# The rounded copy of the attention core moves to ScalarE, with other rearrangements, in an encoder trunk of feed-forward, attention and recurrent layers

## What is computed

```python
for layer in range(2):
    g = norm_gains[layer]
    h = h + 0.5 * rms_norm(swiglu(rms_norm(h, g[0]), ffn_w_in[layer, 0], ffn_w_out[layer, 0]), g[1])
    hn = rms_norm(h, g[2])
    m = attention_mixer(hn, ...) if layer == 0 else recurrent_mixer(hn, ...)
    h = h + rms_norm(m, g[3])
    h = h + 0.5 * rms_norm(swiglu(rms_norm(h, g[4]), ffn_w_in[layer, 1], ffn_w_out[layer, 1]), g[5])
return h[:, 16:]
```

## Time and profile before

| | |
|---|---|
| median of 3 runs | 1040.99 us (1040.65 to 1041.19) |
| the profiled execution | 1041.22 us, of which the span is 1039.3 us |
| PE busy | 1023.8 us, 99% |
| DVE, ACT, POOL busy | 708.7, 562.5, 64.0 us |
| granted TensorE clock | 0.999 |
| read from HBM, written | 167.82 MB, 1.05 MB |

### The profile page before, as it was taken

The page is one execution under the profiler, slowest core; times in us unless marked ns, Lnnn a source line. Parts: engine busy times, 40 slices in busy tenths (PEclk is TensorE's granted clock), DMA queues, the critical chain, the costliest instruction groups (busy, mean ns, idle before and its releaser), DMA issues. The chain is left out here.

```text
span 1039.3 us, 20522 instructions
## 1 busy us (share of the span) xinstructions
PE 1023.8 (99%) x8308; PEld 999.9 (96%) x8308; DVE 708.7 (68%) x1040; ACT 562.5 (54%) x834; POOL 64.0 (6%) x62
## 2 busy tenths in 40 slices
PE   8999999999999999999999999999999999999997
PEld 8999999999889999999999999999999999999886
DVE  6766656488868866655478666654899987676652
ACT  6554454467875644445465444444679865544641
POOL 0000000008004000002100000030000030000000
PEclk9999999999999999999999999999999999999999
DMA  9754446635204355535655654367453736556531
GB/s 294 240 178 161 147 149 205 211 111 174 69 1 163 123 174 187 181 116 190 205 163 162 195 170 141 114 207 226 123 167 97 264 95 208 184 179 233 179 118 41
DMA packets 158175, 170.16 MB, mean 164 GB/s; under 512 B 3344, under 2 KB 150088, under 8 KB 158104
## 3 DMA queue, kind: packets, MB, share of 16 engines
q1 hardware_dynamic: 157720, 168.70, 50.1%
q0 software_dynamic: 96, 0.28, 0.1%
q10 hardware_dynamic: 288, 0.18, 0.1%
HBM read 167.82 MB, written 1.05 MB: 162 GB/s over the span
## 5 line engine op out<-in xcount | busy, mean ns | idle before, releaser
L1591 DVE TENSOR_TENSOR wl<-raw,wh 128x2048 fp32r<-128x2048 f32 (+3 forms) x166 | 346.6, 2108 | 141.5 <-ACT wh L1092 141.2
L508 PE MATMUL bank<-xh,wl 128*128 128x272 f32 (+1 forms) x1492 | 431.6, 289 | 0.2 <-DVE tmp L1707 0.2
L510 PE MATMUL bank<-xh,wh 128*128 128x272 f32 (+1 forms) x1492 | 428.5, 287 | 0.0
L509 PE MATMUL bank<-xl,wh 128*128 128x272 f32 (+1 forms) x1492 | 427.0, 286 | 0.0
L1092 ACT ACTIVATE wh<-raw 128x2048 fp32r<-128x2048 f32 (+2 forms) x165 | 284.2, 1746 | 104.5 <-PE bank L510 83.8
L508 PEld LDWEIGHTS bank<-xh,wl 128*128 128x128 f32 x1492 | 281.1, 188 | 2.1 <-issue 1.2
L510 PEld LDWEIGHTS bank<-xh,wh 128*128 128x128 f32 x1492 | 281.1, 188 | 0.0
L509 PEld LDWEIGHTS bank<-xl,wh 128*128 128x128 f32 x1492 | 281.0, 188 | 0.0
L509 PE MATMUL bank<-al,wh 128*128 128x272 f32 x528 | 152.2, 288 | 0.0
L508 PE MATMUL bank<-ah,wl 128*128 128x272 f32 x528 | 152.2, 288 | 0.0
L510 PE MATMUL bank<-ah,wh 128*128 128x272 f32 x528 | 151.4, 287 | 0.0
(11 more groups left out here) (246 smaller groups left out, 1191.2 us busy)
## 6 DMA issues: line engine op xcount, KB each, us to landing
raw<-in_ffn_w_in SPq DMA_DIRECT2D x87, 1024.0 KB, 5.8
raw<-in_ffn_w_out SPq DMA_DIRECT2D x24, 768.0 KB, 4.7
raw<-in_ffn_w_out SPq DMA_DIRECT2D x24, 640.0 KB, 3.9
raw<-in_ffn_w_out SPq DMA_DIRECT2D x10, 1024.0 KB, 5.0
raw<-in_rec_w_in SPq DMA_DIRECT2D x8, 1024.0 KB, 5.4
raw<-in_attn_w_qkv SPq DMA_DIRECT2D x6, 1024.0 KB, 5.0
raw<-in_attn_w_o SPq DMA_DIRECT2D x4, 1024.0 KB, 5.5
raw<-in_rec_gate_w SPq DMA_DIRECT2D x16, 256.0 KB, 3.7
```

Of the source, the lines that this page charges most:

```text
L508: pe.matmul(dst, b, mh, start=first, stop=False)
L509: pe.matmul(dst, a, ml, start=False, stop=False)
L510: return pe.matmul(dst, a, mh, start=False, stop=last)
L1591: dve.tensor_tensor(wl[:, slot(u), 0:kn * 256], w, wh[:, slot(u), 0:kn * 256].bitcast(F32), ALU.subtract).then_inc(w_ready, units)
```

## The change

Five places change.

1. In the core, DVE's `tensor_copy` of `weighed` goes; ACT makes it (`out_high`), behind `exponents(s+1)` and ahead of `place(s)`; the last one stands ahead of `high(U_WO + 3)`.
2. In projection 1, `mg_first` comes after the fourth bank on both engines, and DVE's last low part comes behind the add of bank 6 instead of ahead of it.
3. In the recurrent block, POOL's `restore(4)` becomes DVE's `restored` in four pieces; the first tap of groups 0 and 1 goes to ACT (`first_tap`); two low parts go ahead of `conv(0)` and `conv(1)`.
4. In `recurrent_out`, squares go to four buffers (`rout_square`: the two of `sqb` and the two of `pad`), with a wait that is looser by two.
5. At the start, tokens come as three loads of whole rows under one semaphore; the first two quarters of unit 0 are issued by ACT ahead of the gains, and ACT's and DVE's order of the first parts follows.

```diff
+def rout_square(m):
+    return (sqb[:, m % 2] if m % 4 > 1 else pad[:, m % 2, 0:L])[:, PROJ_T0[4]:L]
...
 if n == 0:
-    for k0, k1, done in ((0, 2, quarter_landed[0]), (2, 4, quarter_landed[1]), (4, 8, landed[0])):
-        if k0 < 4:
-            tokens(k0 // 2)
-        sp.dma_start(raw[:, 0, 256 * k0:256 * k1].rearrange("p (k c) -> p k c", k=k1 - k0),
-                     vin[:, k0:k1, 0:256]).then_inc(done, 16)
+    sp.dma_start(raw[:, 0, 256 * 4:256 * 8].rearrange("p (k c) -> p k c", k=4), vin[:, 4:8, 0:256]).then_inc(landed[0], 16)
     load(1, 0, KC, vin[:, :, FF:FF + 256])
...
-def tokens(half):
-    cols = slice(D // 2 * half, D // 2 * half + D // 2)
-    sp.dma_start(tok_in[META:TT, 0, cols], x[0:TT - META, cols]).then_inc(s_xin[half], 16)
-    sp.dma_start(tok_in[0:TT, 1, cols], x[TT - META:2 * TT - META, cols]).then_inc(s_xin[half], 16)
-    sp.dma_start(tok_in[0:L - 2 * TT, 2, cols], x[2 * TT - META:SEQ, cols]).then_inc(s_xin[half], 16)
...
+sp.dma_start(tok_in[META:TT, 0, :], x[0:TT - META, :]).then_inc(s_xin, 16)
+sp.dma_start(tok_in[0:TT, 1, :], x[TT - META:2 * TT - META, :]).then_inc(s_xin, 16)
+sp.dma_start(tok_in[0:L - 2 * TT, 2, :], x[2 * TT - META:SEQ, :]).then_inc(s_xin, 16)
 ffn(0)
...
 if c == 0:
-    pe.wait_ge(s_xin[0], 64)
-if c == 4:
-    pe.wait_ge(s_xin[1], 48)
+    pe.wait_ge(s_xin, 64)
 if c >= 4:
...
 for g in range(4):
-    if g == 3:
-        mg_first(pj)
     square_tile(pj, 2 * g, PROJ_BANKS[pj][g][0])
     square_tile(pj, 2 * g + 1, PROJ_BANKS[pj][g][1])
+    if g == 1:
+        mg_first(pj)
     if g < 3:
...
+def out_high(pair):
+    act.wait_ge(pv_done, pair + 1)
+    act.activation(xh[:, pair, :], weighed[:, 0:L], ACT.Copy).then_inc(oh_ready, 1)
...
         exponents(s + 1)
+    if s >= 2 and (s - 2) % STEPS_S:
+        j, i, half = pair_of(s - 2)
+        if half:
+            out_high(2 * j + i)
     place(s)
...
         exponents(s + 2)
+out_high(2 * NKV - 1)
 high(U_WO + 3, 0)
...
+def first_tap(n):
+    act.wait_ge(xr_scaled, 2 * n + 2)
+    for i in range(2):
+        m = 2 * n + i
+        act.activation(xc[:, n, i, :], pad[:, i, 0:L], ACT.Identity, scale=vec_b[:, V_CONVW + m:V_CONVW + m + 1],
+                       bias=vec_b[:, V_CONVB + m:V_CONVB + m + 1]).then_inc(first_tapped, 1)
...
 unit_high("g1", (xr_done, 4), 1)
+first_tap(0)
 unit_high("e0", (xr_done, 6), 1)
 conv_high(0)
+first_tap(1)
 unit_high("e1", (xr_done, 8), 1)
...
 act.wait_ge(proj_done, 8 * 4 + m + 1)
-act.wait_ge(acc_step, ACC * 4 + m + 1)
-act.activation(sqb[:, m % 2, t0:L], rout_dst(m), ACT.Square).then_inc(sq_ready, 1)
+act.wait_ge(acc_step, ACC * 4 + max(2, m - 1))
+act.activation(rout_square(m), rout_dst(m), ACT.Square).then_inc(sq_ready, 1)
 act.activation(mg[:, m, t0:L], rout_dst(m), ACT.Copy, scale=vec_a[:, g:g + 1]).then_inc(mg_ready, 1)
...
-act.dma_start(tok_in[0:META, 0, :], meta).then_inc(s_xin[0], 16)
+act.dma_start(tok_in[0:META, 0, :], meta).then_inc(s_xin, 16)
 act.dma_start(cst[:, 0:C_ROT], consts[:, 0:C_ROT]).then_inc(s_in, 16)
+first_in = ffn_in[0, 0].rearrange("(k p) c -> p k c", p=P)
+for q in range(2):
+    act.dma_start(raw[:, 0, 512 * q:512 * q + 512].rearrange("p (k c) -> p k c", k=2),
+                  first_in[:, 2 * q:2 * q + 2, 0:256]).then_inc(quarter_landed[q], 16)
 act.dma_start(vrow[:, 0, :], gains.rearrange("l i (c p) -> (l i c) p", p=P)).then_inc(s_vin, 16)
...
+high_part(0, 0, 2, (quarter_landed[0], 16), wh_half)
+high_part(0, 2, 4, (quarter_landed[1], 16), wh_half)
 take_h(1)
-high_part(0, 0, 2, (quarter_landed[0], 16), wh_half)
 act.wait_ge(vec_ready, 1)
...
 x_high(0, 2)
-high_part(0, 2, 4, (quarter_landed[1], 16), wh_half)
 x_high(0, 3)
...
 def projection(pj, u0):
-    for g in range(4):
-        if g == 3:
-            mg_first(pj)
+    for g in range(3):
         add_squares(pj, 2 * g)
-        if g < 3:
-            add_squares(pj, 2 * g + 1)
+        add_squares(pj, 2 * g + 1)
+        if g < 2:
             low(u0 + g + 4, 0)
...
             invert_root(pj)
+        if g == 1:
+            mg_first(pj)
+    add_squares(pj, 6)
+    low(u0 + 6, 0)
     residual(pj)
...
 def out_split(pair):
-    dve.wait_ge(pv_done, pair + 1)
-    dve.tensor_copy(xh[:, pair, :], weighed[:, 0:L]).then_inc(oh_ready, 1)
     dve.wait_ge(oh_ready, pair + 1)
...
 dve.wait_ge(xr_scaled, 2 * n + 2)
-for tap in range(CONVW):
+for tap in range(1 if n < TAPPED else 0, CONVW):
     for i in range(2):
...
 else:
-    dve.wait_ge(conv_step, 2 * (CONVW * n + tap) + i - 1)
+    if tap == 1 and n < TAPPED:
+        dve.wait_ge(first_tapped, 2 * n + i + 1)
+    else:
+        dve.wait_ge(conv_step, 2 * (CONVW * n + tap) + i - 1)
     dve.scalar_tensor_tensor(xc[:, n, i, :], pad[:, i, tap:tap + L], vec_b[:, v:v + 1], xc[:, n, i, :],
-                             ALU.mult, ALU.add).then_inc(conv_step, 1)
+                             ALU.mult, ALU.add).then_inc(conv_step, 2 if tap == 1 and n < TAPPED else 1)
...
+def restored(chunks):
+    dve.wait_ge(root_inverted, 4)
+    dve.wait_ge(x_ready, 8 * 4 + 8)
+    dve.wait_ge(hsq_ready, 8 * 4 + 8)
+    for c in chunks:
+        dve.tensor_tensor(h[:, c, PROJ_T0[4]:L], h[:, c, PROJ_T0[4]:L], root[:, PROJ_T0[4]:L], ALU.mult).then_inc(h_restored, 1)
...
 x_scaled(0)
+unit_low("g0", 1)
 conv(0)
-unit_low("g0", 1)
 conv_low(0)
 x_scaled(1)
+unit_low("g1", 1)
 conv(1)
-unit_low("g1", 1)
 conv_low(1)
...
 e_part(1)
+restored(range(0, 3))
 unit_low("e2", 3)
...
 gated_input(3)
+restored(range(3, 5))
 y_gated(0)
...
 e_part(2)
+restored(range(5, 6))
 rout_low(0)
...
 e_part(3)
+restored(range(6, 8))
 rooted(2)
...
 for m in range(7):
-    add_squares(4, m)
+    dve.wait_ge(sq_ready, 8 * 4 + m + 1)
+    dve.wait_ge(acc_step, ACC * 4 + m + 2)
+    dve.tensor_tensor(acc[:, PROJ_T0[4]:L], acc[:, PROJ_T0[4]:L], rout_square(m), ALU.add).then_inc(acc_step, 1)
 residual(4)
...
+low_part(0, 0, 2, (wh_half, 1), w_half)
 copy_h(0)
...
 copy_h(3)
-low_part(0, 0, 2, (wh_half, 1), w_half)
+low_part(0, 2, 4, (wh_half, 2), w_half)
+copy_h(4)
 dve.wait_ge(vec_ready, 1)
...
 low_x(0, 1)
-copy_h(4)
-low_part(0, 2, 4, (wh_half, 2), w_half)
 low_x(0, 2)
...
 pool.wait_ge(hsq_ready, 8 * n + 8)
-if n == 4:
-    pool.wait_ge(y_full, NB)
 for c in range(KC):
```

More of the change, by code:

```diff
@@ L65 @@
 ROUT_SPLIT = 2
+TAPPED = 2
 ROUT_PLAN = [(c, 0, 2) for c in range(KC)] + [(c, 2, 4) for c in range(KC)] + [(c, 4, 6) for c in range(6)] + [(c, 6, 8) for c in range(6)] + [(6, 4, 8), (7, 4, 8)]
@@ L267, in build @@
         gates_used = sem("gates_used")
+        first_tapped = sem("first_tapped")
         xc_rounded, xc_split = sem("conv_rounded"), sem("conv_split")
@@ L271, in build @@
         s_rope = sem("rotary_tables_landed")
-        s_xin = [sem("left_tokens_landed"), sem("right_tokens_landed")]
+        s_xin = sem("tokens_landed")
         quarter_landed = [sem(f"first_unit_quarter{i}_landed") for i in range(2)]
@@ L2238, in _ @@
             restore(3)
-            restore(4)
 _INS = ["x", "meta_tokens", "norm_gains", "ffn_w_in", "ffn_w_out", "attn_w_qkv", "attn_q_gain", "attn_k_gain",
```

## The result

The changed kernel takes 1049.88 us (median of 6 runs, 1049.27 to 1050.84), the kernel before 1041.15 (6 runs): ratio 1.0085, 95% interval 1.0076 to 1.0095. It is slower, as forecast, by 8.7 us where 5.3 were forecast, and lies 0.9 us above the range. The profiled execution took 1050.84 us with a span of 1049.1; it is the slowest of the six, with a mean granted clock of 0.993, where the two fastest (1049.27 and 1049.32) have 0.996. Two executions that are far longer than the others of their kernel (1234.76 us of the kernel before, 5734.86 of filled_waits) are left out of the comparisons.

A forecast was written before the change was run, and what follows sets the result against it. PE, busy 99% of the span, was taken to bound the kernel. The terms 5.1 + 0.4 - 0.9 + 0.7 = +5.3 us gave 1046.3 us beside the median 1040.99, range 1042.4 to 1049.0.

The forecast's parts named there:

- Core, +5.1 forecast: Attention core: ACT's copies start late in six pairs and the delay passes through; +5.1 us, bounds +3.8 and +6.0.
- Projection 1, +0.4: Projection 1: the earlier add's gain is taken by POOL's late restoring; root +0.4 us late, bounds -1.25 and +0.8.
- Recurrent block and output, -0.9: Recurrent block costs nothing; in its output waits for `mg` and `acc` go, smaller ones come; -0.9 us, bounds -1.4 and -0.3.
- First loads, +0.7: Start: transposes wait behind the gains, products begin at 11.4 instead of 10.7 us; +0.7 us, bounds -0.4 and +2.4.
- rival 3: Start: the forecast, but with gains at the late bound, 10.8 us; 1048.0 us in all, chance 0.22.
- plain byte order: Start: 1.75 MB ahead of the gains' end at 249 GB/s take 7.1 us from 2.0, so gains land at 9.1.
- the bound of +2.4: Start: upper bound of the first loads' cost, beside a forecast of +0.7 us.
- The sentence that ACT's high parts don't set the end: Start: ACT's two high parts stand ahead of `take_h(1)`, but their quarters land before the gains.
- the top of the range: Whole kernel: core +6.0, projection 1 +0.8, output -0.4 and loads +1.6 us; 1049.0 us.
- Rival 1: Core: ACT takes the copy at once, PE's 1.4 us wait for `xl` goes; 1037.1 us in all, chance 0.07.

The follow-up runs named there:

- filled_waits: The changed kernel with products that nobody reads, in PE's order ahead of its long waits; 1047.29 us, ratio 1.0060.
- gains_first: The changed kernel with the gains' load issued ahead of the two quarters on ACT's queue; 1051.04 us, ratio 1.0093.
- last_copy_on_dve: The changed kernel with only the eighth copy, the one behind the core, back on DVE; 1048.34 us.
- loads_alone: The kernel before with only the first loads rearranged and ACT's and DVE's new order there; 1044.95 us, ratio 1.0036.
- fourth_copy_early: early_copies_no_loads with the fourth copy, too, ahead of the exponents that follow it in the remainder step; 1038.44 us, ratio 0.9977.
- loads_old_order: The kernel before with whole-row tokens and quarters on ACT's queue behind the gains, ACT and DVE in old order; 1042.61 us, ratio 1.0017.
- copy_alone: The kernel before with only the copy of the weighed values moved to ACT; 1048.32 us, ratio 1.0069.
- copy_early: The changed kernel with ACT's copy ahead of the next exponents instead of behind them; 1046.01 us, ratio 1.0055.
- early_copies_no_loads: The changed kernel with the first loads as before, ACT's copies ahead of the exponents and the eighth copy on DVE; 1041.06 us, ratio 0.9996.

## Why the prediction was wrong

**Core, +5.1 forecast.** The mechanism was right: copies late by 0.91, 0.76, 0.37 and 1.38 us in the first four pairs, where 0.91, 0.87, 0.46 and 1.38 were worked out, and every delay passed through. Alone the copy cost 4.4 us in the core, since each late copy cost up to 0.2 us less than the sum had it. The copy's price, 0.40 by the nearest row, measured 0.393. What the sum lacked is the clock: in the profiled execution the core lost 6.2 us, of which 1.5 to 1.8 are the lower clock's (the core lost 4.7 with the waits filled, 4.4 with the copy alone). In gains_first and last_copy_on_dve, whose core is the same but at the lower clock for half as long, it lost 5.1 and 5.8.

**Projection 1, +0.4.** Right up to the root, where it measured +0.5: the wait for `acc` went, POOL's restoring ended 2.0 us later against the work around it, and PE came to the split chunk 0.5 us later than with the core's shift alone. Wrong behind it: the new wait of 1.9 us was followed by 1.5 us of loss at the lower clock.

**Recurrent block and output, -0.9.** Measured -1.2; cover for the added work was there.

**First loads, +0.7.** This term was mis-sized most: +2.8 in the profiled execution, +4.0 by the median of loads_alone. The gains landed at 10.8, the late bound (rival 3), not at 9.1 (1.75 MB at 249 GB/s are 7.0 us, not 7.1, which weighs nothing here): the step that failed is the choice of plain byte order. The first product came 3.2 us late, more than the bound of +2.4, and 1.0 of that are transposes at the lower clock. The sentence that ACT's high parts don't set the end held, since the quarters were there at 8.40 and 10.25; with the gains early it no longer does, as gains_first shows.

**The range** failed because no term stood for the clock. The trace of before showed it at 1.00 up to PE's last product, and the prediction took each new wait at its length. With the forecast's own late bound for the gains (1048.0) and no other change the time misses 1.9 us, less than the 2.6 us that filled waits gave back; with the waits filled it is 1047.29, inside the range. Nor was the top of the range made of the prediction's own bounds: +1.6 stands there for the loads, whose bound was +2.4, and -0.4 for the output, whose bound was -0.3. With those it would have been 1049.9, and the measured time would have lain just inside by luck, with no clock in the sum. The Trainium skill, "TensorE: Matmul & The Clock Gate", section "HAM oscillation — how this bites in real kernels", tells of waits behind which PE's products start slow again and again. Three stretches at 0.50 here agree, behind waits of 2.3 us and less, which are shorter than those it tells of. **Rival 1** fell: in the changed kernel ACT took the first four copies 0.4 to 1.4 us later than DVE had. Where it takes them at once the core gains, but 0.5 us in fourth_copy_early and not the 1.4 of the rival. The rule of the Trainium skill, "Perfetto Trace Analysis", section "Optimizing Scalar/DVE Operations", on offloading to Scalar was worth no more than that here. The Trainium skill's "Issuing engines are not separate DMA queues", in "DMA: Bandwidth & Descriptors", agrees with loads_old_order: other queue, no earlier landing.

Not settled: why copy_alone and copy_early, with the same waits behind the fourth pair, ran their cores at the full clock in the one execution profiled of each; how often each stretch at the lower clock comes was counted only by the two groups of early_copies_no_loads.

## What to carry to other kernels

When work moves to another engine, look at what stands in front of it in that engine's order at the moment it becomes ready: the same copy cost 4.4 us in the core behind two exponents and nothing ahead of them. Price a new wait of the engine that is 99% busy at more than its length, and leave room in the range for a lower clock behind it. A load or a small step that is moved ahead of another queue's work is late by all that is now in front of it, and taking away one such wait only shows the next.

## What the runs showed that had not been expected

One wait of 1.2 us, behind a first of 0.6, could set some 6 us of the core to 1.2 GHz (early_copies_no_loads: seven of eleven executions some 2 us slower; fourth_copy_early, without that wait: none of eleven), while the same two waits in copy_alone's profiled execution, and a wait of 1.38 us at the start of the kernel before, left the clock at 1.00. Products that nobody reads, put into the waits, kept the clock up and made the changed kernel 2.6 us faster.
